# Weights stationary, tokens moving in the feed-forward up stage and the gated branches

## The chip, the cores and the metric

One Trainium2 chip, of which the kernel uses one core. The metric is the device time of one execution in microseconds, lower is better. The engines are named as in the profile: PE is TensorE's matmuls, PEld its weight loads, DVE VectorE, ACT ScalarE, POOL GpSimd, SP SyncE.

## What is computed

Two transformer blocks, one after the other, on 256 tokens of width 2048, all in float32. What matters here is how the branches are gated and summed, and the feed-forward up stage of the second block:

```python
# block one: three branches u = (attention output * silu(z)) @ w_branch
g = jax.nn.sigmoid(gate_logits.reshape(b, s, N_BRANCHES, D_MODEL))   # rms_norm(x) @ w_in[:, gates]
y = g[:, :, 0] * ua + g[:, :, 1] * ub + g[:, :, 2] * uc
return x + y @ w_out
...
# block two
merged = (jax.nn.sigmoid(ga) * jnp.einsum('bsc,cd->bsd', y_a, w_branch[l, 0])
          + jax.nn.sigmoid(gb) * jnp.einsum('bsc,cd->bsd', y_b, w_branch[l, 1])
          + jax.nn.sigmoid(gm) * jnp.einsum('bsc,cd->bsd', y_m, w_branch[l, 2]))
mix_out = jnp.einsum('bsd,de->bse', merged, w_out[l])
x = x + rms_norm_2(mix_out, norm_mix_post[l])
h2 = rms_norm_2(x, norm_ffn_pre[l])
up_g, up_v = jnp.split(jnp.einsum('bsd,df->bsf', h2, w_ffn_up[l]), 2, axis=-1)
act = jax.nn.gelu(causal_dwconv3(up_g, conv_ffn_w[l]) + conv_ffn_b[l], approximate=True) * up_v
ffn_out = jnp.einsum('bsf,fd->bsd', act, w_ffn_down[l])      # FFN_DIM = 5632
```

`causal_dwconv3` runs along the tokens, per feature. `rms_norm` scales each token; the kernel applies the gain per feature when it splits the activations and the token's scale to the product.

## The kernel before

Weights stream from memory in chunks of 2 x 128 rows by 512 columns (512 KB; some chunks at the end of a stage have one row block). A ring of four slots holds `raw`, `hi` and `lo`. For each chunk SyncE loads `raw`, ScalarE writes `hi` (the value rounded to fp32r), VectorE writes `lo` = raw - hi (L1552), and TensorE multiplies. `convert` on ScalarE and VectorE is called three chunks ahead (`LEAD = 3`), and it waits until TensorE is done with the chunk that last had the slot. Activations are split likewise into high and low parts, transposed so that features lie on partitions (`xh`, `xl`, `oh`, `ol`, `fh`, `fl`). One product is three matmuls: low activation x hi, high activation x hi, high activation x lo.

The stages run in a fixed order that is written out by hand for each engine: `a_proj`, `b_proj`, `c_proj`, the gates of block one (`gate_a`, `gate_b`, `gate_c`), `out`, `mem_kv_2`, `conv_proj`, `mq_proj`, `hg_proj`, the gates of block two (`gate_conv`, `gate_mem`, `gate_hg`), `out_2`, `ffn_first`, `ffn_up`, `ffn_down`. Beside the chunks each engine does side work, keyed by the chunk's number j in a stage's iteration i (`side(i, j)`): on TensorE that is the attention and recurrence products and transposes.

An iteration of a gate stage makes 512 columns of y: block 0 (eight chunks, pair 0) is the gate's logits from x, block 1 (four chunks, pair 1; of sizes 2, 2, 1, 1 in gate_a and gate_b, four of 1 in gate_c and four of 2 in block two) is the branch product. At j = 7 ScalarE writes `sig` = sigmoid(acc[0] x token scale), where in block one the token scale `rnx` is a column per partition; at the last j VectorE multiplies with acc[1] (L1775) and adds into `y` (L1780, L1782), which has tokens on partitions. Ahead of and in the first chunks of `out` and `out_2`, `stepwise` transposes y in eight blocks of 4 (`split`, L681; banks `tp[0]`, `tp[1]`), ScalarE makes oh and VectorE ol (L1575) of each block, and TensorE waits for block j before chunk j.

In `ffn_first` and `ffn_up` an iteration makes 512 features of g (block 0) and of v (block 1). ScalarE evacuates both with the token scale `rnf` (`ffn_ev`); in the next iteration TensorE transposes them (`ffn`, at j = 0, 1, 4, 5), VectorE does the convolution along the tokens from PSUM (L2099, L2102), ScalarE the gelu, VectorE the product with v (L2111), and ScalarE and VectorE split the result into fh and fl. `acc_free`, `chunk_done`, `lo_ready`, `sig_free` are the semaphores between them.

Of the kernel before, what the change touches and what calls it, by code (L numbers as in the profile page):

```python
# [25 lines left out]
F32 = mybir.dt.float32  # L26
# [6 lines left out]
P = 128  # L33
D = 2048
# [129 lines left out]
def two_blocks(  # L164
# [74 lines left out]
    h_ss = const("h_ss", [HH, T])  # L239
    ident = kc[:, K_ID:K_ID + P]  # L240
# [8 lines left out]
    y1 = at("y1", W_AT, [T, D])  # L249
# [61 lines left out]
    y2 = at("y2", W_AT, [T, D])  # L311
# [5 lines left out]
    f_g = at("f_g", F_W, [T, NB])  # L317
    f_v = at("f_v", F_W + 4096, [T, NB])
# [66 lines left out]
    y1_split = Stage(sem, "y1_split", **split_steps(BANKS))  # L385
    y2_split = Stage(sem, "y2_split", **split_steps(BANKS))

    sig_free = sem("sig_free")
    GATES = ("gate_a", "gate_b", "gate_c", "gate_conv", "gate_mem", "gate_hg")
# [10 lines left out]
    for n in range(len(LEVELS) + 1):  # L400
# [3 lines left out]
        if n > 0:  # L404
# [9 lines left out]
    ffs = Stage(sem, "ffs", pe=["g0", "g1", "v0", "v1"], act=["ev", "gelu0", "gelu1", "h"],  # L414
                dve=[f"{k}" for c in range(4) for k in (f"c{c}", f"b{c}1", f"b{c}2")] + ["y", "l"])
# [57 lines left out]
    OUT_SLOTS = [*range(10, 24), 0, 1]  # L473
    OUT2_SLOTS = [*range(0, 8), *range(16, 24)]

    def stationary(name, block):
# [6 lines left out]
        if name.startswith("gate"):  # L483
            if block == 0:
                return xh, xl, own
            first = {"gate_a": 16, "gate_b": 0, "gate_c": 6, "gate_conv": 0, "gate_mem": 16, "gate_hg": 8}[name]
            return oh, ol, lambda k: first + k
        if name == "out":
            return oh, ol, lambda k: OUT_SLOTS[k]
        if name == "out_2":  # L490
            return oh, ol, lambda k: OUT2_SLOTS[k]
# [43 lines left out]
    def gate_used(name, i):  # L535

        return sig_free, 1 + T * (GATES.index(name) * (D // NB) + i + 1)

# [98 lines left out]
    def _(pe):  # L637
# [26 lines left out]
        def stream(side, ready=None):  # L664
            def body(ph, i):
                for j, pos in enumerate(positions(ph)):
                    if ready:
                        ready(i, j)
                    chunk(ph, i, j, pos)
# [20 lines left out]
        def stepwise(st, src, ready, side):  # L690
# [12 lines left out]
            return stream(ahead, have)  # L703
# [5 lines left out]
        def vectors(i, j):  # L709

            if i == 1 and j == 0:
# [4 lines left out]
                ins.then_inc(*setup.mark("pe", "v"))  # L716

# [119 lines left out]
        def for_branch(st, src, ready, at_, side, ready_of=None):  # L837
# [10 lines left out]
            return stream(both, have)  # L848

        pe.wait_ge(*ua_split.after("dve", "l2"))  # L850
        run(pe, "gate_a", stream(late(forget)))
# [35 lines left out]
        run(pe, "gate_b", stream(late(memory)),  # L887
# [3 lines left out]
        run(pe, "gate_c", stream(nothing),  # L891
# [7 lines left out]
        run(pe, "out", stepwise(y1_split, lambda t, c: y1[:, t, c:c + P], lambda n: gate_used("gate_c", n // 2), out_side))  # L899
# [106 lines left out]
        run(pe, "gate_conv", stream(recur(0)))  # L1006
        end_phase(pe, "gate_conv", wait=False)
        run(pe, "gate_mem", stream(recur(4)), last=stream(recur(4)), lasts=2,
            first=for_branch(ym_split, lambda t, c: mq[:, t, c:c + P], ma.after("dve", "u", HH // 2 - 1), [0, 1, 2, 3], recur(4)))
        end_phase(pe, "gate_mem", wait=False)  # L1010
        run(pe, "gate_hg", stream(nothing),
            first=for_branch(yb_split, lambda t, c: hg[:, 3, t, c:c + P], None, [2, 3, 4, 5], nothing, lambda n: hn.after("dve", f"n{n}")))
        end_phase(pe, "gate_hg", wait=False)
        run(pe, "out_2", stepwise(y2_split, lambda t, c: y2[:, t, c:c + P], lambda n: gate_used("gate_hg", n // 2), nothing))
        end_phase(pe, "out_2", wait=False)

        def ffn(i, at_, step):

            st, n = ("g", f_g) if step < 2 else ("v", f_v)
            h = step % 2  # L1020
            pe.wait_ge(*ffs.after("act", "ev", i))
            if step >= 2:
                pe.wait_ge(*ffs.after("dve", f"b{2 * h + 1}2", i))
            for c in range(2):
                for t in range(T):
                    ins = tr(tp[h][:, c * S + t * P:c * S + (t + 1) * P], n[:, t, (2 * h + c) * P:(2 * h + c + 1) * P])
            ins.then_inc(*ffs.mark("pe", f"{st}{h}"))

        def ffn_side(i, j):
            if j in (0, 1):  # L1030
                ffn(i, j, j)
            if j in (4, 5):
                ffn(i, j, j - 2)

# [4 lines left out]
        def down_first(i, j):  # L1039
            ffn_side(FT // 4 - 1, j)  # L1040
# [1126 lines left out]
```

## Time and profile before

| what | value |
|---|---|
| time, median of 3 | 2629.25 us (2628.07 to 2629.6) |
| span of the profiled execution | 2625.2 us |
| PE busy | 2575.0 us, 98%, 11926 records |
| PEld busy | 2123.9 us, 81% |
| DVE busy | 1482.2 us, 56% |
| ACT busy | 1372.7 us, 52% |
| DMA | 482.18 MB, mean 184 GB/s |

The span goes from the first to the last instruction of the profiled execution; the time of a run also has what lies around it. A matmul's recorded duration is its latency: matmuls overlap, so what one costs is read from the starts of two in a row. In the timeline equal instructions in a row are merged, with their count at the end and the time from the first start to the last end.

### The profile page before, as it was taken

To read this page: it belongs to the slowest core of one execution; us is meant where nothing else is said; L and a number is where in the kernel's file an instruction comes from. 1 tells how busy PE (TensorE), PEld (TensorE's weight loads), DVE (VectorE), ACT (ScalarE), POOL (GpSimd) and SP (SyncE) were. 2 spreads that over 40 slices of the span, in tenths; PEclk is the share of its full clock that TensorE was granted. 3 is DMA by queue.
4 is the path that set the end of the run, shared out by engine and by line. 5 is a ranking of instruction groups with operands and counts; after the bars stand their busy time and mean duration, and the time that the engine had idled before them with its cause. 6 is when DMAs were issued, how large, how long until landed. Compare 5 with 4: busy or idle time off the path is not lost.

```text
span 2625.2 us, 34962 instructions
## 1 busy us (share of the span) xinstructions
PE 2575.0 (98%) x11926; PEld 2123.9 (81%) x11926; DVE 1482.2 (56%) x1959; ACT 1372.7 (52%) x1925; POOL 9.0 (0%) x17
## 2 busy tenths in 40 slices
PE   7999999999999999999999999999999999999998
PEld 6788788788878888888888888878788888888886
DVE  4455555555556544445477776555556565665444
ACT  5454655555445544454576665444555455554443
POOL 0000000000000000000000000000000000000000
PEclk9999999999999999999999999999999999999999
DMA  7555565556665666655555555666556656566564
GB/s 259 166 162 168 152 193 164 156 173 179 209 215 181 212 192 192 192 169 176 160 161 169 166 169 163 192 198 218 183 179 190 189 178 192 169 198 221 196 198 148
DMA packets 242763, 482.18 MB, mean 184 GB/s; under 512 B 15138, under 2 KB 15440, under 8 KB 240496
## 3 DMA queue, kind: packets, MB, share of 16 engines
q1 hardware_dynamic: 240240, 462.52, 57.7%
q0 software_dynamic: 2432, 18.46, 2.0%
q8 instruction: 56, 0.92, 0.1%
q14 instruction: 35, 0.29, 0.0%
HBM read 474.62 MB, written 6.30 MB: 183 GB/s over the span
## 4 chain that ended last, share of the span: by engine, by line
PE 96%; ACT 2%; DVE 1%; issue 1%; DMA 0%; DVEq 0%; ACTq 0%; SPq 0%
PE acc L639 89%; PE sc L639 3%; PE tp L643 3%; ACT L1051 0%; ACT hi L1051 0%; DVE lo L1552 0%; DMA x_in<-in_x 0%; DVE x2b L2070 0%; ACT sc L1051 0%; PE sc L643 0%; DVE ssh L1722 0%; ACT b_sq L1051 0%; DVE ol L1575 0%; DVE xl L1573 0%; DVE mem_in L1597 0%
## 5 line engine op out<-in xcount | busy, mean ns | idle before, releaser
L1552 DVE TENSOR_TENSOR lo<-raw,hi 128x1024 fp32r<-128x1024 f32 (+1 forms) x896 | 1066.5, 1195 | 940.1 <-ACT hi L1051 932.0
L1051 ACT ACTIVATE hi<-raw 128x1024 fp32r<-128x1024 f32 (+1 forms) x896 | 924.1, 1036 | 845.6 <-PE acc L639 793.9
L639 PE MATMUL acc<-hi,xl 128*128 128x512 f32 x2368 | 946.8, 400 | 9.5 <-DVE lo L1552 5.3
L639 PE MATMUL acc<-lo,xh 128*128 128x512 f32 x2368 | 926.6, 391 | 0.0
L639 PE MATMUL acc<-hi,xh 128*128 128x512 f32 x2368 | 924.6, 390 | 0.0
L639 PEld LDWEIGHTS acc<-hi,xl 128*128 128x128 f32 x2368 | 446.5, 189 | 106.3 <-issue 13.4
L639 PEld LDWEIGHTS acc<-lo,xh 128*128 128x128 f32 x2368 | 445.9, 188 | 96.4
L639 PEld LDWEIGHTS acc<-hi,xh 128*128 128x128 f32 x2368 | 446.9, 189 | 87.5
L639 PE MATMUL acc<-hi,ol 128*128 128x512 f32 x640 | 256.8, 401 | 5.5 <-DVE ol L1575 5.5
L639 PE MATMUL acc<-lo,oh 128*128 128x512 f32 x640 | 250.5, 391 | 0.0
L639 PE MATMUL acc<-hi,oh 128*128 128x512 f32 x640 | 249.8, 390 | 0.0
L639 PEld LDWEIGHTS acc<-hi,ol 128*128 128x128 f32 x640 | 120.7, 189 | 28.8 <-DVE ol L1575 6.0
L639 PEld LDWEIGHTS acc<-lo,oh 128*128 128x128 f32 x640 | 120.4, 188 | 26.4
L639 PEld LDWEIGHTS acc<-hi,oh 128*128 128x128 f32 x640 | 120.9, 189 | 23.2
L639 PE MATMUL acc<-hi,fl 128*128 128x512 f32 x352 | 137.4, 390 | 0.3 <-issue 0.3
L639 PE MATMUL acc<-lo,fh 128*128 128x512 f32 x352 | 137.0, 389 | 0.0
L639 PE MATMUL acc<-hi,fh 128*128 128x512 f32 x352 | 137.0, 389 | 0.0
L1051 ACT ACT_TABLE_LOAD x85 | 109.1, 1283 | 31.7 <-PE tp L643 10.8
L639 PEld LDWEIGHTS acc<-hi,fl 128*128 128x128 f32 x352 | 66.1, 188 | 14.3 <-issue 0.7
L639 PEld LDWEIGHTS acc<-lo,fh 128*128 128x128 f32 x352 | 66.1, 188 | 13.9
L639 PEld LDWEIGHTS acc<-hi,fh 128*128 128x128 f32 x352 | 66.1, 188 | 13.5
L639 PE MATMUL acc<-hi,m2l 128*128 128x512 f32 x128 | 50.7, 396 | 0.3 <-issue 0.3
(301 smaller groups left out, 1478.5 us busy)
## 6 DMA issues: line engine op xcount, KB each, us to landing
raw<-in_w_in SPq DMA_DIRECT2D x416, 512.0 KB, 3.9
raw<-in_w_ffn_up SPq DMA_DIRECT2D x176, 512.0 KB, 4.4
raw<-in_w_ffn_down SPq DMA_DIRECT2D x80, 512.0 KB, 4.7
raw<-in_w_out SPq DMA_DIRECT2D x64, 512.0 KB, 4.4
raw<-in_w_mem_kv SPq DMA_DIRECT2D x48, 512.0 KB, 4.0
raw<-in_w_branch SPq DMA_DIRECT2D x48, 512.0 KB, 4.1
raw<-in_w_branch_a SPq DMA_DIRECT2D x8, 512.0 KB, 4.8
raw<-in_w_branch_b SPq DMA_DIRECT2D x8, 512.0 KB, 4.8
```

Of the source, the lines that this page charges most:

```text
L639: return nc.tensor.matmul(o, lhsT, rhs, start=start, stop=stop)
L643: return nc.tensor.transpose(o, in_, ident[0:k, :])
L1051: return nc.scalar.activation(o, in_, func, **kw)
L1552: v.tensor_tensor(lo[:, slot, 0:size], raw[:, slot, 0:size], hi[:, slot, 0:size].bitcast(F32), ALU.subtract).then_inc(lo_ready, 1)
```

## The change

In `gate_*`, `ffn_first` and `ffn_up` a new `chunk_by_feature` takes 128 features of the weight chunk as the stationary operand and all 256 tokens as the moving one: four feature blocks with three matmuls of 256 columns each, where `chunk` had two token halves with three of 512. The results have features on partitions. So y, g and v need no transposes: `y1`, `y2` and `sig` are laid out by feature, y's high and low parts are made 1024 elements per partition at a time, for iteration i - 1 at j = 2 (ScalarE, `y_hi`) and j = 3 (VectorE, `y_lo`) of iteration i of the last gate stage and for the last one after it. The token scale is now along the free dimension: TensorE makes a row of it in every partition (ones x diagonal of the scales), once for `rnx` in `a_proj` and once for `rnf` in `ffn_first`. In gate_a to gate_c VectorE multiplies acc[0] by that row into `sig` and ScalarE takes the sigmoid of `sig` (before: ScalarE alone, from PSUM). In the up stage VectorE evacuates g with the row, convolves from SBUF within the same iteration, multiplies the gelu by the row, and at the start of the next iteration multiplies it by v straight from acc[1]; TensorE has no side work there. `stationary` and the slots of oh and ol are adapted.

```diff
@@ TensorE
+        def chunk_by_feature(ph, i, j, pos):
...
+            for kk in range(size):
+                ks = place(k0 + kk)
+                for m in range(4):
+                    feat = slice(m * P, (m + 1) * P)
+                    o = acc[pair][m // 2][:, (m % 2) * S:(m % 2 + 1) * S]
+                    end = last and kk == size - 1
+                    opens = k0 + kk == 0 and m % 2 == 0
+                    nc.tensor.matmul(o, hi[:, slot, kk, feat], al[:, ks], start=opens, stop=False, skip_group_check=True)
+                    nc.tensor.matmul(o, hi[:, slot, kk, feat], ah[:, ks], start=False, stop=False, skip_group_check=True)
+                    ins = nc.tensor.matmul(o, lo[:, slot, kk, feat], ah[:, ks], start=False, stop=end, skip_group_check=True)
...
+            if (i, j) == (0, 9):
+                pe.wait_ge(*x_row.after("dve", "d"))
+                for t in range(T):
+                    ins = mm(sc[1][:, t * P:(t + 1) * P], kc[:, K_ONE:K_ONE + P], x_diag[:, t])
+                ins.then_inc(*x_row.mark("pe", "r"))
...
+        def y_ready(st):
+            def have(i, j):
+                if j < BANKS and j % 2 == 0:
+                    pe.wait_ge(*st.after("dve", "l", j // 2))
+            return have
-        run(pe, "out", stepwise(y1_split, lambda t, c: y1[:, t, c:c + P], lambda n: gate_used("gate_c", n // 2), out_side))
+        run(pe, "out", stream(out_side, y_ready(y1_split)))
...
-        run(pe, "ffn_up", stream(ffn_side))
+        run(pe, "ffn_up", stream(nothing, one=chunk_by_feature))
@@ ScalarE
+                if j == KT // 2 - 1 and name in ("gate_a", "gate_b", "gate_c"):
+                    for h in range(2):
+                        act.wait_ge(acc_free[0], 2 * ph.use(i, 0) + h + 1)
+                        go(sig[:, h], sig[:, h], ACT.Sigmoid).then_inc(sig_ready, 1)
...
+        def y_hi(st, name, y, n):
+
+            act.wait_ge(*gate_used(name, n))
+            go(oh[:, bass.ds(n * 4 + Y_SLOT, 4)], y[:, bass.ds(n * 4, 4)]).then_inc(*st.mark("act", "h"))
...
+        def ffn_side(i, j):
+            if j == 1:
+                ffn_hi(i)
+            if j in (10, 11):
+                ffn_act(i + 1, j - 10)
@@ VectorE
+                if j == KT // 2 - 1 and scaled:
+                    dve.wait_ge(*x_row.after("dve", "r"))
+                    dve.wait_ge(*gate_used(ph.name, i - 1))
+                    dve.wait_ge(chunk_done, ph.chunk(i, j) + 1)
+                    for h in range(2):
+                        v.tensor_tensor(sig[:, h].rearrange("p (a b) -> p a b", a=2), acc[0][h][:].rearrange("p (a b) -> p a b", a=2),
+                                        x_r[:].unsqueeze(1).to_broadcast([P, 2, S]), ALU.mult).then_inc(acc_free[0], 1)
...
+        def ffn_gate(ph, i, it):
+
+            dve.wait_ge(chunk_done, ph.chunk(i, KT // 2 - 1) + 1)
             for h in range(2):
-                dve.wait_ge(*ffs.after("pe", f"v{h}", i))
+                v.tensor_tensor(f_g[:, 2 * h:2 * h + 2], acc[0][h][:].rearrange("p (a b) -> p a b", a=2), by_token(2),
+                                ALU.mult).then_inc(acc_free[0], 1)
...
+        def ffn_scale(it):
+            dve.wait_ge(*ffs.after("act", "gelu1", it))
+            v.tensor_tensor(f_a[:], f_a[:], by_token(4), ALU.mult).then_inc(*ffs.mark("dve", "s"))
+
+        def ffn_mul(before, it):
+
+            dve.wait_ge(chunk_done, before + 1)
+            dve.wait_ge(*ffs.after("dve", "s", it))
+            for h in range(2):
                 part = f_a[:, 2 * h:2 * h + 2].rearrange("p a b -> p (a b)")
-                ins = v.tensor_tensor(part, part, tp[h][:], ALU.mult)
-            ins.then_inc(*ffs.mark("dve", "y"))
...
+                v.tensor_tensor(part, part, acc[1][h][:], ALU.mult).then_inc(acc_free[1], 1)
+            dve.drain().then_inc(*ffs.mark("dve", "y"))
...
         def ffn_side(i, j):
...
+            if j == 0:
+                ffn_mul(ph.chunk(i, -1), i)
+            if j == 2:
                 ffn_lo(i)
+            if j == 8:
+                ffn_gate(ph, i, i + 1)
+            if j in (9, 10):
+                ffn_conv(i + 1, j - 9)
+            if j == 12:
+                ffn_scale(i + 1)
```

## Rows read from the trace of the kernel before

**Rows 1.** The page: busy time of each engine, and the chain that ended last.

```profile
PE 2575.0 (98%) x11926; PEld 2123.9 (81%) x11926; DVE 1482.2 (56%) x1959; ACT 1372.7 (52%) x1925; POOL 9.0 (0%) x17
...
PE 96%; ACT 2%; DVE 1%; issue 1%; DMA 0%; DVEq 0%; ACTq 0%; SPq 0%
```

**Rows 2.** The page, costliest groups: busy us, mean ns; idle before, releaser.

```profile
L1552 DVE TENSOR_TENSOR lo<-raw,hi 128x1024 fp32r<-128x1024 f32 (+1 forms) x896 | 1066.5, 1195 | 940.1 <-ACT hi L1051 932.0
L1051 ACT ACTIVATE hi<-raw 128x1024 fp32r<-128x1024 f32 (+1 forms) x896 | 924.1, 1036 | 845.6 <-PE acc L639 793.9
L639 PE MATMUL acc<-hi,xl 128*128 128x512 f32 x2368 | 946.8, 400 | 9.5 <-DVE lo L1552 5.3
```

**Rows 3.** Timeline (start us, us, engine line op), matmuls, loads; then chain of waits.

```profile
2449.89 0.39 PE L639 MATMUL acc<-hi,fh 128*128 128x512 f32 x1
...
2451.02 0.39 PE L639 MATMUL acc<-hi,fl 128*128 128x512 f32 x1
...
2449.89 0.19 PEld L639 LDWEIGHTS acc<-lo,fh 128*128 128x128 f32 x1
...
950.62 0.44 issue
951.06 130.86 PE acc L639 x576
```

**Rows 4.** Timeline of the forget-gate projection: matmuls, then one of its loads.

```profile
270.13 0.28 PE L639 MATMUL sc<-xh,wf_lo 128*12 128x256 f32 x1
...
271.88 0.28 PE L639 MATMUL sc<-xh,wf_lo 128*12 128x256 f32 x1
...
275.51 0.28 PE L639 MATMUL sc<-xl,wf_hi 128*12 128x256 f32 x1
...
270.13 0.09 PEld L639 LDWEIGHTS sc<-xh,wf_hi 128*12 128x12 f32 x1
```

**Rows 5.** Timeline: eight matmuls merged, then three wide loads merged.

```profile
544.23 1.05 PE L639 MATMUL sc<-mk,c_pt 128*128 128x128 f32 x8
...
1334.66 0.41 PEld L639 LDWEIGHTS sc<-h_g 128*128 128x128 f32 x3
```

**Rows 6.** Up stage: timeline of transposes and matmuls; tile f_g's evacuations (ns min/median/max).

```profile
1964.00 0.60 PE L643 MATMUL tp<-kc,f_g 128*128 128x128 f32 x4
...
1967.21 0.60 PE L643 MATMUL tp<-kc,f_g 128*128 128x128 f32 x4
...
L1051 ACT ACTIVATE f_g<-acc,rnf x22: 681/686/690, 1894.3 to 2349.4; 128x512 f32<-128x512 f32 x22
```

**Rows 7.** Both out stages' starts: timeline of PE, then DVE, windows and waits.

```profile
758.96 0.39 PE L639 MATMUL acc<-lo,oh 128*128 128x512 f32 x1
...
767.95 0.60 PE L643 MATMUL tp<-kc,y 128*128 128x128 f32 x4
...
1763.76 0.39 PE L639 MATMUL acc<-lo,oh 128*128 128x512 f32 x1
...
1770.56 0.60 PE L643 MATMUL tp<-kc,y 128*128 128x128 f32 x4
...
761.46 1.29 DVE L1782 TENSOR_TENSOR y<-y,sig 128x512 f32 x2
...
763.00:767.00 4.00, 3.31 (x8) 2.65 (x9) 2.43 (x5) 0.00 (x0) 0.71 (x1) 0.57 1.00 365
...
PE acc L639 <- DVE ol L1575: 5.5, 2, 3.2
```

**Rows 8.** Timeline: four fp32 records of 128 columns.

```profile
1331.48 0.60 PE L639 MATMUL sc<-qt,h_k 128*128 x4
```

**Rows 9.** An iteration of gate_c: ScalarE and VectorE in the timeline.

```profile
699.63 1.27 ACT L1051 ACTIVATE sig<-acc,rnx 128x512 f32<-128x512 f32 x2 [2.17 <-PE acc L639]
...
701.45 0.69 DVE L1552 TENSOR_TENSOR lo<-raw,hi 128x512 fp32r<-128x512 f32 x1 [3.26 <-ACT hi L1051]
```

**Rows 10.** Windows, up stage: PE, PEld, DVE, ACT, POOL busy; clock, DMA share, GB/s.

```profile
1916.00:2371.00 455.00, 454.74 (x2081) 375.92 (x2081) 272.92 (x310) 243.29 (x271) 0.00 (x0) 1.00 0.60 184
```

More of the change, by code:

```diff
@@ L662, in chunk, with stream @@
             ins.then_inc(chunk_done, 1)
-        def stream(side, ready=None):
+        def chunk_by_feature(ph, i, j, pos):
+            blk, k0, size, last = pos
+            pair = blk % 2
+            slot = (ph.c0 + j) % RING
+            ah, al, place = stationary(ph.name, blk)
+            if k0 == 0 and not (isinstance(i, int) and ph.use(i, blk) == 0):
+                pe.wait_ge(acc_free[pair], 2 * ph.use(i, blk))
+            pe.wait_ge(lo_ready, ph.chunk(i, j) + 1)
+            for kk in range(size):
[8 more added lines that the diff above has]
+                    ins = nc.tensor.matmul(o, lo[:, slot, kk, feat], ah[:, ks], start=False, stop=end, skip_group_check=True)
+            ins.then_inc(chunk_done, 1)
+        def stream(side, ready=None, one=chunk):
             def body(ph, i):
@@ L668, in body @@
                         ready(i, j)
[L669 removed]
+                    one(ph, i, j, pos)
                     side(i, j)
@@ L702, in have @@
                     pe.wait_ge(*st.after("dve", f"l{j}"))
-            return stream(ahead, have)
+            return stream(ahead, have, one)
         pe.wait_ge(in_first, 16 * 2)
@@ L847, in have, with gate @@
                     pe.wait_ge(*st.after("dve", f"l{len(at_) - 1}"))
-            return stream(both, have)
+            return stream(both, have, chunk_by_feature)
+        def gate(side):
+            return stream(side, one=chunk_by_feature)
         pe.wait_ge(*ua_split.after("dve", "l2"))
-        run(pe, "gate_a", stream(late(forget)))
+        run(pe, "gate_a", gate(late(forget)))
         end_phase(pe, "gate_a", wait=False)
@@ L885, in memory_first @@
             memory(i, j - 1)
-        run(pe, "gate_b", stream(late(memory)),
+        run(pe, "gate_b", gate(late(memory)),
             first=for_branch(ub_split, lambda t, c: pb[:, t, 3 * BW + c:3 * BW + c + P], fg.after("dve", "u", D // NB - 1),
@@ L890, in _ @@
         end_phase(pe, "gate_b", wait=False)
-        run(pe, "gate_c", stream(nothing),
+        run(pe, "gate_c", gate(nothing),
             first=for_branch(uc_split, lambda t, c: pc[:, t, CW + c:CW + c + P], me.after("dve", "u", D // NB - 1), [0, 1], nothing))
@@ L1012, in _ @@
             first=for_branch(yb_split, lambda t, c: hg[:, 3, t, c:c + P], None, [2, 3, 4, 5], nothing, lambda n: hn.after("dve", f"n{n}")))
         end_phase(pe, "gate_hg", wait=False)
[L1014 removed]
+        run(pe, "out_2", stream(nothing, y_ready(y2_split)))
         end_phase(pe, "out_2", wait=False)
[L1017 to L1024, printed above, removed]
[L1025 to L1027 removed]
@@ L1765, in gate_side @@
         def gate_side(ph, y, first, more=None):
+            scaled = ph.name in ("gate_a", "gate_b", "gate_c")
             def side(i, j):
@@ L1783, in gate_side, with y_lo_before, side @@
+        def y_lo_before(st, y, more):
+            def side(i, j):
+                if j == 3 and not (isinstance(i, int) and i == 0):
+                    y_lo(st, y, i - 1)
+                if more:
+                    more(i, j)
             return side
```

229 lines of the change are left out of this document (126 added, 103 removed).

## The prediction

> **What bounds the kernel now.** I read the page first. TensorE is busy 98% of the span and the chain that ended last is 96% TensorE [rows 1]; VectorE and ScalarE stand at 56% and 52%. So only two things can move the end: the pace of the weight-streaming matmuls, and what stands between them on TensorE's queue. The costliest groups [rows 2] show what kind of matmuls: 128x512 moving, each with a 128x128 weight load, in threes (hi with low activations, hi with high, lo with high). Their 390 ns is one instruction's latency, not its cost. The cost is the distance between two starts: in the timeline of the down stage 2449.89 to 2451.02 holds five of them, 0.226 us each, and in the chain of waits 576 matmuls of a stage without side work take 130.86 us; without the last one's tail (0.39 - 0.23) that is 130.7 / 576 = 0.2269, and over shorter stretches 0.2267, which I use [rows 3]. All 10,464 of them take 10,464 x 0.2267 = 2372 us of the 2625.2; the other 253 us are side work and stalls, and that is where a gain must come from, while the pace is where a loss could come from.
>
> **The swap itself.** A k-step had 2 token halves x 3 matmuls of 512 columns; it gets 4 feature blocks x 3 of 256. The streamed columns stay at 3072, but the weight loads go from 6 to 12. Counting k-steps in the code: gate_a and gate_b 88 each, gate_c 80, the three gates of block two 96 each, the up stage 352, together 896. So 5376 matmuls of 0.2267 us (1219 us) become 10,752 of 256 columns, whose pace the trace has to give. Break-even on the pace alone is half the old one, 0.1133 us.
>
> Two neighbours bound it. (a) The forget-gate projection runs 48 matmuls of 256 moving columns in the same type, back to back: the first fifteen steps go from 270.13 to 271.88, 0.1167 us each, the rest to 275.51 at 0.1135 each [rows 4]. That is 512 columns' pace halved, but its loads are narrow (128x12, 0.09 us). (b) Full 128x128 loads back to back: the timeline merges eight of them before 128-column matmuls, whose starts lie (1.05-0.27)/7 = 0.111 us apart, and three before 64-column ones, (0.41-0.19)/2 = 0.110 apart [rows 5]. A load is thus a matter of 0.110 to 0.112 us once loads overlap; its recorded 0.19 is again latency. Under 512 columns each load starts as the matmul before it starts (2449.89 in both views [rows 3]), so it lies in the shadow of the stream, and will need 0.111 of the 0.1133 available. Also, 512-column matmuls with wide loads run at the same rate per column as 256-column ones with narrow loads, so the load costs the stream nothing. I take 0.1133, the row that has the same type and width; surplus zero. Ends for the range: 0.1133 below (never seen faster per column in this type, so no gain) and 0.1167 above, 10,752 x 0.0034 = 36 us.
>
> The Trainium skill speaks against the change here: "TensorE: Matmul & The Clock Gate", section "Back-to-back issue gap", says that in a stream of load and matmul pairs the spacing is set by both, and its section on LDWEIGHTS puts a load at its columns over 1.2 GHz. By that, as an estimate, a load is 107 ns against 107 ns of streaming, a tie that could go to either side. The trace has 0.111 against 0.1133, so here the stream just wins. What a load slightly longer than the stream would do is in rivals B and C, worked out from rows.
>
> **What is removed from TensorE.** (1) The transposes of the up stage. Per iteration g and v are each transposed in two blocks of four; in 11 iterations (22 evacuations of g) that is 44 blocks [rows 6]. One block with the twelve matmuls behind it takes 1964.00 to 1967.21 = 3.21 us against 12 x 0.2267 = 2.72: 0.49 us, of which 0.36 are the transposes and the rest is a first matmul that is late and ten uneven ones. 44 x 0.49 = 21.6 us. Nothing hides them: they are on TensorE's own queue and it is never waiting.
> (2) The transposes of the branch sum y, 64 of them, 16 blocks [rows 7]. Two blocks stand ahead of each out stage, with a stall: the sum's last column is finished by VectorE only after the last gate block, and the split of y queues behind it (two waits on ol, 5.5 us together). From the last gate matmul to the block after the first chunk: 758.96 to 767.95 = 8.99 us, against 13 x 0.2267 = 2.95, so 6.04; in block two 1763.76 to 1770.56, 3.85. The first is dearer because its idle time drops the granted clock to half (0.57 over 763 to 767). Then six more blocks each, 12 x 0.49 = 5.9. A change of stage with nothing to wait for costs some 0.4 us ("issue", 0.44 in rows 3), and stays: 6.04 + 3.85 + 5.9 - 0.8 = 15.0 us. What is late next there: ScalarE must wait for the last quarter of y before it converts chunk 3 of the out stage. In the trace VectorE ends that sum at 761.46 + 1.29 = 762.8 [rows 7] and TensorE ended the gate stage at 758.96 + 0.23 = 759.2; 1.04 for y's high part, 1.04 for hi and 1.20 for lo [rows 2] end at 766.1, and three chunks of 2.72 last until 767.4. No stall, 1.3 us to spare.
>
> **What is added.** (3) Two rows of token scales (ones times a diagonal), two fp32 matmuls each, four records; the like of it is four records in 0.60 us of h_k, 0.36 of it queue time [rows 8]. With its tail 0.5 each: 1.0 us. The wait for VectorE's diagonal is met: ScalarE reads the final rnf from 1894.3 on, with the eighth chunk's result [rows 6], and the ones product stands a chunk later. (4) VectorE in gate_a to gate_c: two PSUM products, some 0.65 us each as y's sums in rows 7, at the eighth chunk, which ScalarE's sigmoids now wait for, with the hi conversions queued behind the sigmoids and TensorE waiting for them in the end. Tightest in gate_c, whose branch chunks last 1.36 us. There block 0 ends at 699.5, the sigmoids run 699.63 to 700.9, lo of the fourth chunk behind block 0 starts at 701.45 [rows 9] and is wanted by the load at 699.35 + 3 x 1.36 - 0.23 = 703.2. With the products ahead: first product to 700.3, sigmoids to 701.7, hi (some 0.6 for a chunk of one row block) to 702.3, lo with its 0.69 to 703.0. That leaves 0.2 us; I book 0.2 us lost in each of 4 iterations, 0.8 us, with 0 and 2 us as ends. gate_a and gate_b have two chunks of 2.72 in the same place and cover it. (5) y's split in blocks of 1024 columns on ScalarE and VectorE replaces sixteen pairs of smaller pieces and lies beside streaming. (6) In the up stage ScalarE's four evacuations (0.686 each [rows 6]) go and VectorE gets two PSUM products, a scale and two PSUM products instead of two; the convolution now reads SBUF. VectorE is busy 272.92 us of 455 there [rows 10], so some 2 us more in each 43.5 us iteration is covered. Cost nothing; if that cover went, up to 20 us. (7) Loop ends, now with the same count of queued matmuls but half their time: today none shows a gap. Ten iterations of the up stage fill 455 us [rows 10], and 1920 x 0.2267 + 40 x 0.49 = 454.9, so nothing is lost at their ends. 0 to 2 us, I take 0.
>
> **Sum.** 21.6 + 15.0 - 1.0 - 0.8 - 0 = 34.8 us off the profiled execution, span 2625.2 to 2590.4. The median 2629.25 lies 4.05 us above the span (launch and end around it), so 2594.5; I say 2595 us, -1.3%.
>
> **Rivals.** A: as above, 2588 to 2603 with 0.1133 to 0.1137 us per matmul. B: the pace sits at the uneven 0.1167 of the first fifteen steps in rows 4, because every chunk boundary or side block restarts it: +36 us, 2631, no measurable change; in between, a load that must end before the next matmul may start and starts 0.0035 late (within the 0.01 us to which rows 3 show both starts as one) makes 0.1145 and +13 us, 2608. For it: no row has wide loads and 256 columns in this type together, and in rows 6 ten matmuls after each block are uneven. Against: unevenness ends by itself after some 2 us in each case, and costs 12 columns' worth there, already in the 0.49. C, the slower side: weight loads become the bound. It decides from 0.1133 + 34.8/10,752 = 0.1166 us per matmul. No row has a wide load and a 256-column stream of this type reading at once without pause; if each load is slowed by the stream to 0.120, that is 10,752 x 0.0067 = +72 us, 2667, and if a matmul had to wait out the load's recorded 0.188 it would be 2595 + 10,752 x 0.075 = 3400. Against: in rows 5 eight pairs ran at 0.111. D: VectorE and ScalarE hold TensorE in the gates and the up stage (items 4 and 6 at their worst, 2 + 20 us, 2616). E: transposes go, but the stall ahead of the out stages comes back at the last quarter of y: +5 us, 2600, inside A's range. The clock is no rival of its own: it was full but for two or three stretches, one of which goes.
>
> **Chances.** A (with E) 0.70, the in-between and D 0.10, B 0.06, C 0.14. About 0.2% is what a measurement can tell from no change, so faster means below 2624, slower above 2634.5: faster 0.79, same 0.07, slower 0.14. The range 2587 to 2631 takes in the upper bound of the matmul pace and leaves C out above.
>
> **What would show it.** Right: in the up stage matmul starts 0.1133 us apart with their loads shadowed, an iteration of 43.5 instead of 45.45 us, the weight loads' busy share near 100% there, from 375.92 of 455 us; no transposes of y, f_g, f_v; no idle time at the two starts of the out stages and one clock drop less; the other stages unchanged. The step on pace is wrong if starts lie 0.115 or more apart; the step on cover is wrong if TensorE waits for lo in the gates. The forecast is wrong above all if one number, 0.1133, is off by 3%.

## The result: 1.0% slower

| | before | changed |
|---|---|---|
| median, us | 2629.2 (2628.1 to 2629.6, 4 runs) | 2653.8 (2653.6 to 2654.6, 4 runs) |
| ratio | | 1.0099 (95%: 1.0087 to 1.0111) |
| span of the profiled execution, us | 2625.2 | 2652.8 |
| TensorE matmul records | 11,926 | 17,070 |

A second set of runs of the changed kernel, on the chip of the last kernel below, gave 2654.1 us against 2627.0 for the kernel before (1.0100, 1.0085 to 1.0116). The forecast was 2595 us and a range up to 2631, so both its sign and its range were wrong. An iteration of the up stage, forecast at 43.5 us, takes 46.12 (45.50 before).

The page of the changed kernel: busy time by engine, then the chain that ended last, then groups (busy us, mean ns | idle before, releaser).

```profile
PE 2608.6 (98%) x17070; PEld 2384.5 (90%) x17070; DVE 1511.9 (57%) x1998; ACT 1321.8 (50%) x1838; POOL 9.0 (0%) x17
...
PE 95%; ACT 2%; DVE 1%; issue 1%; DMA 1%; SPq 0%; ACTq 0%; DVEq 0%
...
L1582 DVE TENSOR_TENSOR lo<-raw,hi 128x1024 fp32r<-128x1024 f32 (+1 forms) x896 | 1068.9, 1195 | 936.4 <-ACT hi L1075 931.5
L1075 ACT ACTIVATE hi<-raw 128x1024 fp32r<-128x1024 f32 (+1 forms) x896 | 924.0, 1035 | 966.8 <-PE acc L684 483.0
L682 PE MATMUL acc<-xl,hi 128*128 128x256 f32 x2944 | 842.8, 286 | 2.9 <-issue 1.5
L684 PE MATMUL acc<-xh,lo 128*128 128x256 f32 x2944 | 833.7, 283 | 0.0
L682 PEld LDWEIGHTS acc<-xl,hi 128*128 128x128 f32 x2944 | 565.5, 192 | 7.6 <-issue 4.4
```

Against rows 1 and 2: TensorE is still the bound (98%, 95% of the chain), VectorE and ScalarE have hardly moved, and their conversions are as long as before. PEld went from 81% to 90%. TensorE waits at no place at which it did not wait before, so the loss must be in the pace. The timeline of the up stage, matmuls and then their loads, shows it:

```profile
1999.82 0.28 PE L684 MATMUL acc<-xh,lo 128*128 128x256 f32 x1
1999.94 0.28 PE L682 MATMUL acc<-xl,hi 128*128 128x256 f32 x1
2000.06 0.28 PE L683 MATMUL acc<-xh,hi 128*128 128x256 f32 x1
...
2001.14 0.28 PE L683 MATMUL acc<-xh,hi 128*128 128x256 f32 x1
...
1999.94 0.19 PEld L683 LDWEIGHTS acc<-xh,hi 128*128 128x128 f32 x1
2000.06 0.19 PEld L684 LDWEIGHTS acc<-xh,lo 128*128 128x128 f32 x1
```

From 1999.94 to 2001.14 are ten matmuls: 0.1200 us each, and each load starts with a matmul. The window over the stage (us, PE, PEld, DVE, ACT, POOL busy, clock, DMA share, GB/s) says the same without a pause:

```profile
1940.00:2399.00 459.00, 459.00 (x3827) 459.00 (x3827) 285.20 (x340) 194.17 (x210) 0.00 (x0) 1.00 0.61 182
```

459 / 3827 = 0.1199 us per matmul at full clock, VectorE with 174 us to spare. Per 512 columns that is 0.240 where [rows 3] have 0.2267. PEld is busy all the time, as the prediction had it, but at this slower pace.

The stages of the two traces, each from its first weight-streaming matmul to that of the next, give the account. The second column counts 0.00667 us (0.1200 - 0.1133) for each matmul of 256 columns; the last is what is left of the difference.

| stage | change, us | by the pace | left |
|---|---|---|---|
| gate_a, gate_b | +5.3, +5.7 | 2112 x 0.00667 = 14.1 | -3.1 |
| gate_conv, gate_mem | +5.9, +5.8 | 2304 x 0.00667 = 15.4 | -3.7 |
| gate_c and the start of out | +2.2 | 960 x 0.00667 = 6.4 | -4.2 |
| out | -4.3 | 0 | -4.3 |
| gate_hg and the start of out_2 | +4.1 | 1152 x 0.00667 = 7.7 | -3.6 |
| out_2 | -3.0 | 0 | -3.0 |
| ffn_first, ffn_up, start of ffn_down | +1.9, +6.3, -1.9 | 4224 x 0.00667 = 28.2 | -21.9 |
| all (unrounded) | +27.8 | 71.7 | -43.9 |

The other stages differ by 0.7 us at most. So the change did save what it was to save, and more; the pace cost 72 us. The second column takes the pace of the up stage for all stages; in the gates the median distance of two starts in a row is 0.120 us too.

### The profile page after: what moved, and what is told of

The parts are those of the page before. It is cut to its first block, busy times and chain, and to the rows that moved or that the text cites. A ratio compares the mean times of both kernels' runs of the same rounds, so it can differ in the third digit from the quotient of the medians.

```text
span 2652.8 us, 45120 instructions
## 1 busy us (share of the span) xinstructions
PE 2608.6 (98%) x17070; PEld 2384.5 (90%) x17070; DVE 1511.9 (57%) x1998; ACT 1321.8 (50%) x1838; POOL 9.0 (0%) x17
## 4 chain that ended last, share of the span: by engine, by line
PE 95%; ACT 2%; DVE 1%; issue 1%; DMA 1%; SPq 0%; ACTq 0%; DVEq 0%
PE acc L641 41%; PE acc L682 16%; PE acc L683 16%; PE acc L684 16%; PE sc L641 3%; PE tp L645 2%; DMA raw<-in_w_in 1%; ACT hi L1075 1%; ACT L1075 0%; DVE lo L1582 0%; ACT sc L1075 0%; SPq L545 0%; DVE x2b L2134 0%; PE sc L645 0%; DVE ssh L1760 0%
## 5 line engine op out<-in xcount | busy, mean ns | idle before, releaser
L682 PE MATMUL acc<-xl,hi 128*128 128x256 f32 x2944 | 842.8, 286 | 2.9 <-issue 1.5
L684 PE MATMUL acc<-xh,lo 128*128 128x256 f32 x2944 | 833.7, 283 | 0.0
L683 PE MATMUL acc<-xh,hi 128*128 128x256 f32 x2944 | 833.6, 283 | 0.0
L682 PEld LDWEIGHTS acc<-xl,hi 128*128 128x128 f32 x2944 | 565.5, 192 | 7.6 <-issue 4.4
L683 PEld LDWEIGHTS acc<-xh,hi 128*128 128x128 f32 x2944 | 565.7, 192 | 0.1
L684 PEld LDWEIGHTS acc<-xh,lo 128*128 128x128 f32 x2944 | 565.3, 192 | 0.0
L641 PE MATMUL acc<-hi,xl 128*128 128x512 f32 x896 | 358.5, 400 | 6.6 <-DVE lo L1582 4.9
L641 PE MATMUL acc<-lo,xh 128*128 128x512 f32 x896 | 350.7, 391 | 0.0
L641 PE MATMUL acc<-hi,xh 128*128 128x512 f32 x896 | 350.2, 391 | 0.0
L641 PEld LDWEIGHTS acc<-hi,xh 128*128 128x128 f32 x896 | 169.5, 189 | 33.1
```

What stands on the lines that cost most here:

```text
L641: return nc.tensor.matmul(o, lhsT, rhs, start=start, stop=stop)
L682: nc.tensor.matmul(o, hi[:, slot, kk, feat], al[:, ks], start=opens, stop=False, skip_group_check=True)
L683: nc.tensor.matmul(o, hi[:, slot, kk, feat], ah[:, ks], start=False, stop=False, skip_group_check=True)
L684: ins = nc.tensor.matmul(o, lo[:, slot, kk, feat], ah[:, ks], start=False, stop=end, skip_group_check=True)
```

## Do the parts add up? The up stage alone, the gates alone

```diff
@@ up stage alone, against the changed kernel
-        run(pe, "gate_a", gate(late(forget)))
+        run(pe, "gate_a", stream(late(forget)))
...
@@ gates alone, against the changed kernel
-        run(pe, "ffn_up", stream(nothing, one=chunk_by_feature))
+        run(pe, "ffn_up", stream(ffn_side))
```

(with the work of the other engines that belongs to each, as before the change).

> Only the up stage swapped, the gates, y and the out stages as before. Additive theory (pace 0.120 against 0.1133, and what the transposes cost): 384 + 3840 = 4224 matmuls x 0.00667 = +28.2 us, minus 44 blocks x 0.49 = 21.6 and some uneven matmuls, plus 0.5 for the row; the two traces of before and after give +1.9 in the first iteration, +6.3 in the other ten and -1.9 at the start of the down stage, so +6.3 us, 2635.5. Rival: the gates and the up stage share something (clock, ring of slots, loads) and the parts don't add up: then this is at or below 2629, and the gates alone carry all of the loss.

Measured: 2633.9 us (2630.2 to 2636.4) against 2626.5 (2621.2 to 2629.6), ratio 1.0033 (1.0019 to 1.0047).

> Only the gates swapped, with y by feature and its split pass by pass; the up stage as before. Additive theory: 6528 matmuls x 0.00667 = +43.5 us, minus 15.1 for y's transposes and the stalls at both out stages, minus some 6.7 that side blocks cost less between 256-column matmuls in gate_a, gate_b, gate_conv and gate_mem; the measured 24.6 us less the up stage's 6.3 is +18.3 us, 2647.5. Rival as in the run of the up stage alone: another split of the 24.6 us, by more than 2 us.

Measured: 2647.3 us (2646.8 to 2647.6) against the same 2626.5, ratio 1.0082 (1.0065 to 1.0099). The expectations were +6.3 and +18.3 us; the medians differ by +7.5 and +20.8. The kernel before varied by 8 us on this chip, so these medians say no more than that each part alone loses and that the loss is nearly the sum. The traces are sharper. With the up stage alone, its ten iterations take 461.21 us, as in the changed kernel, and gate_a takes 145.18 as before (before: 145.20; changed: 150.48). With the gates alone, gate_conv takes 156.34 as in the changed kernel (before: 150.49) and the ten iterations 454.95 as before. The traces show nothing that the parts share; each carries its own loss.

## Is it the weight load? Half the weight columns

```diff
+                    w = P if k0 + kk == 0 else P // 2
-                    nc.tensor.matmul(o, hi[:, slot, kk, feat], al[:, ks], start=opens, ...)
+                    nc.tensor.matmul(o[0:w], hi[:, slot, kk, m * P:m * P + w], al[:, ks], start=opens, ...)
```

and so for the other two products. Half of the features get only the first k-step of each sum, so the output is incomplete.

> The changed kernel with half the weight columns: all swapped matmuls but those of each block's first k-step take 64 of 128 features as weights, so output is missing for the other half of the features. Same count, same moving columns, same work on all other engines. Theory L (the full load sets the pace): 9912 of 10,752 matmuls go from 0.120 to 0.1133, -66 us, 2588, and the remaining costs are those of the prediction. Theory F (a fixed cost of each matmul, or the count of instructions, or reads of memory by the moving side): no change, 2654. If the cost grows with the load's columns without a threshold: 0.1167, 2621.

Measured: 2590.6 us (2589.3 to 2592.2), ratio to before 0.9867 (0.985 to 0.9883). Its timeline in the up stage and the window over it:

```profile
1999.81 0.28 PE L685 MATMUL acc<-xh,lo 128*64 128x256 f32 x1
1999.92 0.28 PE L683 MATMUL acc<-xl,hi 128*64 128x256 f32 x1
...
2000.94 0.28 PE L683 MATMUL acc<-xl,hi 128*64 128x256 f32 x1
...
1937.00:2370.00 433.00, 432.75 (x3656) 426.75 (x3655) 277.52 (x324) 192.36 (x205) 1.25 (x2) 1.00 0.63 200
```

From 1999.81 to 2000.94 are ten matmuls: 0.113 us each. The ten iterations take 437.4 us instead of 461.2. So the width of the weights makes the difference between 0.120 and 0.1133 at 256 columns; the number of instructions, the moving side and the other engines are the same. (Half the weight columns are also half the partitions of the result; no run parts the two.) With nearly the pace that I had assumed the kernel is 35.9 us below the kernel before on the same chip, where I had booked 34.8. That they agree so well is in part luck: the 840 matmuls of the first k-steps still cost 840 x 0.00667 = 5.6 us more, so the rest of the change saves more than I had booked, as the account above has it. Theory F had no change here (2654), theory L 2588. I took this at first for a proof of theory L. The bench didn't bear that out.

## The pace by itself: two benches

Behind the last matmul of the changed kernel, into banks that nothing reads any more:

```diff
+        def pace(w, n):
+            for k in range(60):
+                nc.tensor.matmul(tp[(k // 3) % 2][0:w, 0:n], hi[:, k % RING, (k // 4) % 2, 0:w],
+                                 fh[:, 2 * (k % 16):2 * (k % 16) + 2].rearrange("p a b -> p (a b)")[:, 0:n], start=True, stop=True)
+        for n in (512, 480, 448, 416, 384, 352, 320, 304, 288, 272, 256, 248, 240, 232):
+            pace(128, n)
```

The first bench had 42 matmuls for each pair of widths, the second, shown here, 60. Each is one execution, read from its trace.

> The changed kernel with a bench appended to TensorE's queue behind the last matmul of the down stage: for each pair of widths 42 fp32r matmuls back to back, each with its own weight load, into two banks that nothing reads any more. The output is that of the changed kernel; only the time behind the end is more, and isn't what is read. Theory L (a load that lasts longer than the stream sets the pace: a 128-column load takes 0.120 us while matmuls stream, and the stream alone 0.2267 / 512 = 0.4427 ns a column): 128-column weights give 0.120 per matmul at 256 moving columns and the same 0.120 (0.110 at the least) at 224, 192, 160, 128 and 64; 288 gives 0.1275, 320 0.1417, 384 0.170, 448 0.198, 512 0.2267; weights of 96 columns and fewer give 0.1133 at 256. Theory F (each matmul with a full load pays a fixed 13.3 ns beside N columns at 2.4 GHz, 0.4167 ns each, whatever the load hides behind): 512 gives 0.2267, 448 0.200, 384 0.1733, 320 0.1467, 288 0.1333, 256 0.120, 224 0.1067, 192 0.0933, 128 0.0667 (or the 0.110 of the densest loads in the trace as floor), and weights of 64 columns give 0.1133 or less at 256 and less than 0.2267 at 512. A pair of a 512 and a 256-column matmul: 0.3467 by either. 256 columns with a 128-column load and then with a 64-column load in turn: L 0.2333 to 0.24 a pair, F 0.2333.

> A second bench behind the changed kernel, 60 fp32r matmuls for each pair of widths. The first bench fits neither theory whole; what it leaves is theory S (sum with a floor): a matmul takes N x 0.4167 ns plus a handover that depends on the width of the load (13.3 ns with 128 columns, 9.4 with 96, 6.7 with 64 and fewer), and never less than 0.1113 us with a 128-column load. For 128-column weights S gives 0.2267 at 512, 0.2133 at 480, 0.200 at 448, 0.1867 at 416, 0.1733 at 384, 0.160 at 352, 0.1467 at 320, 0.1400 at 304, 0.1333 at 288, 0.1267 at 272, 0.120 at 256, 0.1167 at 248, 0.1133 at 240, 0.1113 at 232. For 64-column weights 0.220 at 512, 0.1667 at 384, 0.140 at 320, 0.1267 at 288, 0.1133 at 256, 0.100 at 224; for 96 columns at 256 0.116, for 112 0.118, for 80 0.1147. Theory L (0.120 for a full load, or 0.4427 ns a column for the stream, whichever is longer) gives 0.120 flat from 232 to 264, 0.1275 at 288, 0.155 at 352, 0.184 at 416, and for 64 columns 0.2267 at 512, 0.170 at 384, 0.1275 at 288, 0.0992 at 224. Four matmuls of 512 columns and then four of 256: by S 4 x (0.2267 + 0.120) = 1.387; if each change between the two lengths costs the 0.006 seen in the strict alternation, 1.393 to 1.40.

In the groups of the second bench (weights as rows*columns, moving operand, count | busy us, mean ns of one) the busy time runs from the first start to the last end, so (busy - one) / 59 is the distance, good to 0.001 us:

```profile
L1073 PE MATMUL tp<-fh,hi 128*64 128x512 f32 x60 | 14.0, 392 | 0.0
L1073 PE MATMUL tp<-fh,hi 128*128 128x512 f32 x60 | 13.8, 389 | 0.0
L1073 PE MATMUL tp<-fh,hi 128*128 128x384 f32 x60 | 10.6, 334 | 0.0
L1073 PE MATMUL tp<-fh,hi 128*64 128x384 f32 x60 | 10.6, 336 | 0.0
L1073 PE MATMUL tp<-fh,hi 128*128 128x320 f32 x60 | 9.0, 309 | 0.0
L1073 PE MATMUL tp<-fh,hi 128*128 128x256 f32 x60 | 7.3, 283 | 0.0
L1073 PE MATMUL tp<-fh,hi 128*96 128x256 f32 x60 | 7.1, 278 | 0.0
L1073 PE MATMUL tp<-fh,hi 128*64 128x256 f32 x60 | 7.0, 276 | 0.0
L1073 PE MATMUL tp<-fh,hi 128*128 128x232 f32 x60 | 6.9, 274 | 0.0
```

(13.8 - 0.389) / 59 = 0.227, (10.6 - 0.334) / 59 = 0.174, (9.0 - 0.309) / 59 = 0.147, (7.3 - 0.283) / 59 = 0.119, (6.9 - 0.274) / 59 = 0.112. The other engines and the DMAs stand nearly still meanwhile (columns as in the window above), so the 0.120 needs neither their load nor the kernel's data flow:

```profile
2645.00:2890.00 245.00, 245.00 (x1621) 222.69 (x1620) 3.91 (x6) 0.00 (x0) 0.00 (x0) 1.00 0.03 9
```

The distances of the starts themselves, in ns, means over the last 49 of each (of the first bench over all 41), beside columns / 2.4 GHz:

| moving columns | 512 | 448 | 384 | 352 | 320 | 288 | 256 | 240 | 224 | 160 | 128 |
|---|---|---|---|---|---|---|---|---|---|---|---|
| columns / 2.4 GHz | 213.3 | 186.7 | 160.0 | 146.7 | 133.3 | 120.0 | 106.7 | 100.0 | 93.3 | 66.7 | 53.3 |
| 128-column weights | 226.7 | 202.7 | 173.4 | 161.1 | 146.7 | 131.7 | 120.0 | 112.0 | 111.4 | 111.3 | 111.4 |
| above it | 13.4 | 16.0 | 13.4 | 14.4 | 13.4 | 11.7 | 13.3 | 12.0 | | | |
| 64-column weights | 230.0 | 202.2 | 173.4 | | 146.7 | 129.9 | 113.3 | | 103.3 | | 59.9 |
| above it | 16.7 | 15.5 | 13.4 | | 13.4 | 9.9 | 6.7 | | 10.0 | | 6.6 |

(Under 256 moving columns, weights of 112, 96, 80 and 64 columns give 117.8, 116.1, 113.3 and 113.3. One and the same weights, moving operand and bank for all 42 matmuls, 128 columns wide, give 120 too.)

What follows:
- Theory L falls. A full load is a floor of 0.1113 us, met only from 232 columns down (64-column weights go below it: 0.103 and 0.060 us); it isn't 0.120 (0.112 at 240 columns). And the stream isn't 0.4427 ns a column: 384 columns take 0.1734, not 0.170, and 320 take 0.1467, not 0.1417.
- Theory F is nearer with full loads, 11 to 17 ns above the columns at 2.4 GHz from 512 down to 240 columns (the ends are 304 columns with 137.7 and 480 with 216.6). But it has no place for the half weight columns, which gain 6.7 ns at 256 columns, 2 at 288, nothing at 320 and 384, and lose 3 at 512.
- Theory S, which joined the two, has most of the values within 3 ns but not that the gain of narrow loads ends at 320, nor the 0.230 of narrow loads at 512.
- 256 columns with a full and a half load in turn take 0.240 a pair, as two full ones. The run of 64 moving columns went from 0.111 to 0.213 halfway, where the granted clock fell from 1.00 to 0.50 (0.50 over 2731 to 2735 us of the first bench): there the floor of a full load is 0.213.
- Four matmuls of 512 columns and then four of 256 take 1.403 us in the second bench, where 4 x (0.2267 + 0.120) is 1.387 and 1.393 to 1.40 was expected.

So a matmul with its own load pays some 13 ns beside its columns, once per matmul and not per column, and cutting 512 columns in two pays it twice. Narrow weights under short streams are the exception: 6.6 to 10 ns with 64 columns under 128 to 288 moving ones, and at 256 exactly the half of 13.3. That exception was the neighbour in [rows 4].

## Can the loads be had back? Two products in one matmul

If the cost is one per matmul, fewer and longer matmuls should win it back. In the up stage PSUM has room for it: the low and the high activations lie behind one another, so hi weights can meet both in one matmul of 512 columns, into a bank for each feature block; VectorE adds the halves. This holds for all but the first block of `ffn_first`. The gates are as before the change.

```diff
-                    nc.tensor.matmul(o, hi[:, slot, kk, feat], al[:, ks], ...)
-                    nc.tensor.matmul(o, hi[:, slot, kk, feat], ah[:, ks], ...)
+                    nc.tensor.matmul(bank[:].rearrange("p (a b) -> p a b", a=2), hi[:, slot, kk, feat], xhl[:, :, ks], ...)
-                    ins = nc.tensor.matmul(o, lo[:, slot, kk, feat], ah[:, ks], ...)
+                    ins = nc.tensor.matmul(bank[:, 0:S], lo[:, slot, kk, feat], ah[:, ks], ...)
...
+                ins = v.tensor_reduce(dst[:, m], wide[pair][m][:].rearrange("p (a s) -> p s a", a=2), AX, ALU.add)
```

> The up stage alone swapped (gates as before), and there the products of hi weights with low and high activations as one matmul of 2 x 256 = 512 moving columns into a bank of its own for each feature block, then lo weights with 256 columns, in turn; VectorE adds the two halves of a bank. Per k-step 4 loads of each instead of 12 loads. From the bench a pair in turn takes 0.353: per k-step 1.413 against 1.440, 344 k-steps, -9.3 us against the run with the up stage alone (2633.9): 2624.6, about as the kernel before on the same chip (-0.1%). Theory L would have 0.3467 a pair, -18.3 us, 2615.6. Rival: VectorE's four reductions of 512 columns and four more, some 4 us per iteration more, hold TensorE at the start of an iteration or the conversions: then at or over 2634.

> As the run before it, but within a k-step first the four matmuls of 512 columns and then the four of 256. If the 0.0065 of a pair in turn belongs to the change of length, two changes per k-step instead of eight remain: 1.387 + 0.01 = 1.397 per k-step, -15 to -18 us against the up stage alone, 2616 to 2619, so 0.3% to 0.4% under the kernel before and under both kernels. If it belongs to each matmul whatever its neighbour: as in turn, 2624.6.

> As the grouped run, but over a whole chunk: eight matmuls of 512 columns, then eight of 256. In the grouped run's trace the three 512-column matmuls that follow one of their own length take 0.2336 and the one before a 256-column one 0.2283, where the down stage has 0.2267; the 256-column ones take 0.1186. If the slower 512 is an after-effect of the change of length that ends after four or five matmuls, as in the first bench (42 of them after 12-column weights took 27 ns too long in all), a chunk saves up to 2 x 22 - 27 = 17 ns: 172 chunks, -2.9 us, 2619.5. If it's a property of the 2 x 256 pattern or of these operands, no change: 2622.5.

> The changed kernel as it is, on the chip of the pair kernels, so that both stand against the same runs of the kernel before: 2653.8, +1.0%; the pair kernels then are 1.1% to 1.2% below it.

(Counted in the code, 336 k-steps and 168 chunks are paired, not the 344 and 172 of the expectations; that changes them by 0.4 us at most.)

| kernel | median, us | ratio to before (95%) | ten iterations of the up stage |
|---|---|---|---|
| before | 2628.2 (with the first two pairs), 2627.0 (with the others) | 1 | 454.95 |
| changed (second set) | 2654.1 (2652.9 to 2654.9) | 1.0100 (1.0085 to 1.0116) | 461.21 |
| pair in turn | 2623.9 (2621.0 to 2628.0) | 0.9987 (0.9978 to 0.9996) | 452.69 |
| grouped in a k-step | 2622.5 (2619.9 to 2624.0) | 0.9980 (0.9971 to 0.9989) | 449.48 |
| grouped over a chunk | 2619.9 (2615.7 to 2621.5) | 0.9969 (0.9957 to 0.9980) | 447.35 |

Timelines of the three, in that order (merged where alike, with the count at the end):

```profile
2099.80 0.40 PE L682 MATMUL tp<-xhl,hi 128*128 128x512 f32 x1
2100.04 0.28 PE L684 MATMUL tp<-xhl,lo 128*128 128x256 f32 x1
2100.16 0.40 PE L682 MATMUL tp<-xhl,hi 128*128 128x512 f32 x1
2100.40 0.28 PE L684 MATMUL tp<-xhl,lo 128*128 128x256 f32 x1
2100.51 0.40 PE L682 MATMUL acc<-xhl,hi 128*128 128x512 f32 x1
```

```profile
2099.90 0.63 PE L682 MATMUL acc<-xhl,hi 128*128 128x512 f32 x2
2100.37 0.62 PE L682 MATMUL sc<-xhl,hi 128*128 128x512 f32 x2
2100.83 0.40 PE L685 MATMUL acc<-xhl,lo 128*128 128x256 f32 x2
2101.07 0.40 PE L685 MATMUL sc<-xhl,lo 128*128 128x256 f32 x2
2101.30 0.63 PE L682 MATMUL acc<-xhl,hi 128*128 128x512 f32 x2
```

```profile
2100.93 0.63 PE L679 MATMUL acc<-xhl,hi 128*128 128x512 f32 x2
...
2102.32 0.62 PE L679 MATMUL sc<-xhl,hi 128*128 128x512 f32 x2
2102.77 0.40 PE L683 MATMUL acc<-xhl,lo 128*128 128x256 f32 x2
...
2103.72 0.63 PE L679 MATMUL acc<-xhl,hi 128*128 128x512 f32 x2
```

In turn, a pair takes 2100.51 - 2100.16 = 0.35 us: 0.236 to the start of the short one, 0.117 to the next. That is more than 0.2267 + 0.120, as the bench had it. Grouped in a k-step, four and four take 2101.30 - 2099.90 = 1.40, and over a chunk 2103.72 - 2100.93 = 2.79 for twice as much. Over the ten iterations a k-step takes 1.415, 1.405 and 1.398 us in the three kernels; 1.397 was expected of the second, whose 2622.5 us miss the 2616 to 2619 of the expectation. The mean distances behind the eight 512-column matmuls of a chunk are 233, 236, 228, 233, 231, 227, 227 and 227 ns: the first five after the short ones are slower, then the pace is that of [rows 3]. Grouping over a chunk brought what its first alternative had (2619.9, expected 2619.5). The ranges of neighbours in this table overlap; the order of the three rests on the traces. VectorE's extra work holds nothing: it is busy 297 us of 400 here, and TensorE has no gap in the window:

```profile
1960.00:2360.00 400.00, 400.00 (x2294) 352.00 (x2293) 297.07 (x359) 171.88 (x187) 0.00 (x0) 1.00 0.62 188
```

The last kernel is 0.3% faster than the kernel before and 1.3% faster than the changed one. Stage by stage its trace is 7.6 us shorter than that of before in the ten iterations, 1.9 at the start of the down stage and 1.2 in `b_proj` (which both kernels have alike), but 1.9 longer in `ffn_first`, 1.2 in `out` and 1.6 in `out_2`, where the clock stands at half for 6.8 and 3.4 us (before: 3.4 and none). Why the clock does so there isn't known. The gates had no room for it: their side work uses the other four banks.

## Why the prediction was wrong, step by step

**The pace: wrong, and it alone turned the sign.** The step that failed is "0.1133, the row that has the same type and width; surplus zero", with its reason that 512-column matmuls with wide loads run at the same rate per column as 256-column ones with narrow loads, "so the load costs the stream nothing". The runs show 0.120 us in its place: 10,752 x 0.00667 = 71.7 us that stood in the sum as nothing. Two points lay on a line through zero by accident: 512 columns with 13.4 ns on top, and 256 columns with 6.7 ns on top, which holds only for narrow loads. Both are 0.4427 ns a column, and neither is a rate. The end that I put above, 0.1167, was again a row of narrow loads and so no bound.

The trace of before did hold the row that would have warned. At the start of ffn_first TensorE had been busy for 1.97 us of 6, and then the clock stands at half. Two windows of before, then matmuls of its timeline, then those of after at the same place:

```profile
1860.00:1866.00 6.00, 1.97 (x8) 1.57 (x8) 4.84 (x10) 3.10 (x8) 0.00 (x0) 0.70 0.10 37
1866.00:1872.00 6.00, 5.55 (x14) 4.29 (x15) 3.80 (x7) 1.39 (x2) 0.00 (x0) 0.50 0.30 87
...
1868.32 0.63 PE L639 MATMUL acc<-hi,xh 128*128 128x512 f32 x1
1868.75 0.63 PE L639 MATMUL acc<-lo,xh 128*128 128x512 f32 x1
```

```profile
1888.43 0.41 PE L684 MATMUL acc<-xh,lo 128*128 128x256 f32 x1
1888.64 0.41 PE L682 MATMUL acc<-xl,hi 128*128 128x256 f32 x1
```

At 1.2 GHz 512 columns take 0.427 us (0.4266 on average), which is 512 / 1.2 with nothing on top, and 256 columns 0.213. (That 0.213 is also the floor of a full load at half clock in the first bench, so it is the 512 columns that tell.) At 2.4 GHz the columns of the first would be 0.2133, and 0.2267 was measured. So 13.4 ns of each matmul at full clock weren't columns. Whether they go with the columns or with the matmul was open, and by the matmul they make 0.120 at 256 columns: a rival with a reason of its own, at 2595 + 71.7 = 2667 us, that deserved far more than 14%.

The Trainium skill gives the isolated gap in "TensorE: Matmul & The Clock Gate", section "Back-to-back issue gap", as the columns over 2.4 GHz plus about 2.5 ns. It has the right form, a part per matmul, but in these streams of fp32r pairs that part is 13 ns. For streams of pairs the same section has some 131 ns at 512 columns, where 226.7 is measured here. Its section on LDWEIGHTS puts a load at its columns over 1.2 GHz, by which an estimate for 128 columns is 107 ns, against the 111.3 measured at full clock.

**Rival C: right price, other mechanism.** It had 0.120 for a load slowed by the stream. The bench shows 0.112 at 240 columns, so no load of 0.120; what is 0.120 is 256 columns and the part per matmul. C's 2667 is 13 us above the result mostly because the saved parts were larger than booked (some 9 us).

**(1) Transposes of the up stage: right.** Booked 21.6 us. The account leaves -21.9 with the row for the scale in it, so some 22.4.

**(2) Transposes of y and the stalls: right.** Booked 15.0; 4.2 + 4.3 + 3.6 + 3.0 = 15.1. The start of out in the changed kernel, TensorE, VectorE, the window over 776 to 780, ScalarE:

```profile
776.07 0.28 PE L684 MATMUL acc<-oh,lo 128*128 128x256 f32 x1
776.61 0.47 PE L641 MATMUL acc<-hi,ol 128*128 128x512 f32 x1 [0.26 <-DVE lo L1582]
776.91 0.40 PE L641 MATMUL acc<-hi,oh 128*128 128x512 f32 x1
...
778.77 1.29 DVE L1832 TENSOR_TENSOR y<-y,sig 128x512 f32 x2
...
776.00:780.00 4.00, 3.74 (x18) 3.01 (x18) 4.00 (x6) 0.02 (x1) 0.00 (x0) 1.00 0.93 263
...
780.09 1.06 ACT L1075 ACTIVATE oh<-y 128x1024 fp32r<-128x1024 f32 x1 [4.07 <-DVE y L1832]
```

From the last gate matmul to the first of out are 0.54 us; in [rows 7] two blocks of transposes and two waits lay there. The clock is full over 776 to 780 (1.00, where rows 7 have 0.57). y's last column comes at 780.06, 3.9 us after TensorE's last gate matmul (3.6 in the trace of before), and still no chunk of out waits for it: out's 91.4 us are 384 x 0.2267 and its own side work. Rival E didn't show. Part of the saving in block one hangs on the clock: in the trace of the up stage alone, whose start of out is as before, the clock doesn't fall there and out takes 94.4 us instead of 95.8.

**(3) Rows of scales: small as booked.** In the timeline thirteen starts around the row in a_proj lie 0.46 us further apart than at the pace, and around the one in ffn_first 0.44; booked 0.5 each. (a_proj is 0.65 us longer as a whole, but 0.44 in the trace of the up stage alone, which has no row there.)

**(4) Products in gate_a to gate_c: covered, and the 0.8 us weren't needed.** No matmul of these three stages waited for lo. The one such wait of a 256-column matmul is at the start of gate_conv, and there the trace of before has the same 0.45 us. The row of waits, then the timeline:

```profile
PE acc L682 <- DVE lo L1582: 0.4, 1, 0.4
...
1337.20 0.38 PE L682 MATMUL acc<-xl,hi 128*128 128x256 f32 x1 [0.45 <-DVE lo L1582]
```

**(5) to (7): right.** No wait appeared in the up stage, nor at loop ends; rival D didn't show.

**Not booked: side work between 256-column matmuls is cheaper.** In gate_a, gate_b, gate_conv and gate_mem 6.8 us are left in the account that no step of mine has. In gate_a the 28 blocks of side work cost in both kernels nearly the same up to the first matmul behind them (21.5 and 21.0 us in all), but the matmuls that follow lose 4.0 us to unevenness before and 2.7 after. In the four stages together the blocks go from 64.0 to 63.2 us and the unevenness from 17.9 to 11.9. That is read from the two traces; I made no run for it.

In sum I had -34.8 us for all but the pace, the traces have -43.9 (and +0.4 in a_proj and b_proj): the missing 6.8 us of side work, the 0.8 of (4) and some 0.8 of (1) are most of the difference. The pace is +71.7 instead of 0. One reading beside the sum was off too: of the 4.05 us between the span of before and its median, launch and end make only some 1.8, as nearly every run with its own span shows (2654.6 against 2652.8 in the changed kernel). The rest is that the profiled execution of before was a fast one by some 2.2 us, which is why the spans differ by 27.6 us and the medians by 24.6.

## What to carry to other kernels

A price per column must not be taken from one width: before cutting long matmuls in two, find two widths with full weight loads, or a stretch at half clock, and split the distance of starts into columns and a part per matmul. Here that part is some 13 ns for fp32r at full clock, so one matmul of 512 columns is 13 ns cheaper than two of 256, and in the up stage four blocks of transposes per iteration (4 x 0.49 = 1.96 us) were cheaper than 384 matmuls at 6.7 ns more each (2.56 us). Where two products share their weights, one matmul over both is the way to have fewer and longer ones, and matmuls of one length belong together.

## What the runs showed that I had not expected

- At full clock (2.4 GHz) a matmul with its own 128x128 fp32r load costs columns / 2.4 GHz plus 11 to 17 ns between 240 and 512 columns, and 0.1113 us at the least; at half clock 512 columns take 0.427 us with nothing on top, and a full load is a floor of 0.213 us.
- Narrower weights help only under short streams: 256 columns go from 120.0 to 117.8, 116.1 and 113.3 ns with 112, 96 and 80 weight columns, 320 and 384 columns don't change with 64, and 512 columns get slower (226.7 to 230.0). Why isn't known; no run here tells it.
- Lengths in turn cost extra: 512 and 256 columns by turns 0.353 us a pair, against 0.3467 for the sum of both alone. In the last kernel it wears off after five 512-column matmuls.
- Weights and moving operand that fill only 64 rows change nothing: 0.120 us (median) at 256 columns, where 64 weight columns give 0.1133.
